# Turns, weight copies, head norms and final stores reordered in a three-block transformer kernel

## The reference, cut to what matters

```python
def first_block(x, ...):                       # blocks 1 and 2 (layers 0 and 1)
    for i in range(2):
        hn = rmsnorm(h, norm_mix[i])
        mix = diff_attention(hn, ...) if i == 0 else neighborhood_attention(hn, ...)
        h = h + mix
        h = h + swiglu(rmsnorm(h, norm_ffn[i]), w_gate, w_up, w_down)     # hidden 2816
        gate = sigmoid(rmsnorm(h, norm_ple[i]) @ ple_w_gate[i])
        h = h + gate * (p[i] @ ple_w_proj[i])
...
# in diff_attention: two softmax maps a head, a[0] - lam * a[1], then
    o = rmsnorm(o, subln) * (1.0 - lam_init)   # a norm per head of 128 values ("head norms")
    return o.reshape(B, S, D_MODEL) @ w_o
...
def second_block(x, meta_tokens, ...):         # block 3
    h = concat([meta, x])                      # 16 meta tokens ahead of the 256
    q, k, v, f_logit, b_gate, c_gate, u = split(rms_norm(h) @ w_in)
    y_attn = forgetting_attention(q, k, v, log_f)             # 8 heads of 64
    y_conv = b_gate * causal_depthwise_conv(c_gate * u, conv_w)    # width 3
    y = concat([head_rms_norm(y_attn), head_rms_norm(y_conv)])
    h = h + y @ w_out
    h = h + square(relu(rms_norm(h) @ w_ff1)) @ w_ff2         # hidden 4096
    return rms_norm(h)[:, 16:]
```

## Time and profile before

| | before |
|---|---|
| time, median of 3 runs | 1049.91 us (1049.12 to 1051.7) |
| profiled execution | 1049.74 us |
| its span in the trace | 1047.8 us |
| mean granted clock of TensorE | 0.989 |
| PE busy | 1004.1 us, 5549 matmuls |
| VectorE, ScalarE busy | 643.9 us, 497.6 us |
| moved by DMA | 174.78 MB, mean 167 GB/s |

### The profile page before, as it was taken

The page is one execution under the profiler, slowest core; times in us unless marked ns, Lnnn a source line. Parts: engine busy times, 40 slices in busy tenths (PEclk is TensorE's granted clock), DMA queues, the critical chain, the costliest instruction groups (busy, mean ns, idle before and its releaser), DMA issues.

```text
span 1047.8 us, 13887 instructions
## 1 busy us (share of the span) xinstructions
PE 1004.1 (96%) x5549; PEld 857.5 (82%) x5549; DVE 643.9 (61%) x990; ACT 497.6 (47%) x728; POOL 126.4 (12%) x207
## 2 busy tenths in 40 slices
PE   6998799999999999999999999999999899999996
PEld 5988678888888898887888888888889778888885
DVE  6766667655566775554665555578654777555553
ACT  6465445444443655454544444455654354444431
POOL 5000399620000000000000000012500000000000
PEclk9899899999999999999999999999999999999998
DMA  9833368956556454333376655545642237555510
GB/s 268 279 121 123 89 150 197 272 193 201 167 195 196 159 190 159 121 121 95 133 239 196 193 176 194 198 138 176 202 145 97 81 121 244 197 164 197 192 50 40
DMA packets 112575, 174.78 MB, mean 167 GB/s; under 512 B 5944, under 2 KB 73536, under 8 KB 112512
## 3 DMA queue, kind: packets, MB, share of 16 engines
q1 hardware_dynamic: 106224, 165.69, 49.5%
q0 software_dynamic: 6272, 8.21, 3.3%
q10 hardware_dynamic: 16, 0.00, 0.0%
HBM read 172.83 MB, written 1.05 MB: 166 GB/s over the span
## 4 chain that ended last, share of the span: by engine, by line
PE 79%; DVE 10%; ACT 6%; issue 3%; DMA 1%; SPq 0%; DVEq 0%; ACTq 0%
PE bank L902 24%; PE bank L904 24%; PE bank L903 24%; DVE wl L1358 4%; ACT wh L582 2%; PE bank L1090 2%; ACT prob L658 1%; PE bank L1012 1%; DMA raw<-in_da_w_qkv_dram 1%; DVE prob L1463 1%; PE bank L917 1%; PE bank L1067 1%; PE bank L1042 1%; ACT pt L675 1%; DVE xl L1426 1%
## 5 line engine op out<-in xcount | busy, mean ns | idle before, releaser
L1358 DVE TENSOR_TENSOR wl<-raw,wh 128x2048 fp32r<-128x2048 f32 x154 | 355.4, 2314 | 229.2 <-ACT wh L582 229.1
L582 ACT ACTIVATE wh<-raw 128x2048 fp32r<-128x2048 f32 x154 | 292.0, 1910 | 107.5 <-PE bank L904 102.1
L902 PE MATMUL bank<-wh,xh 128*128 128x512 f32 (+1 forms) x792 | 302.0, 381 | 5.7 <-DVE xl L1426 4.8
L903 PE MATMUL bank<-wl,xh 128*128 128x512 f32 (+1 forms) x792 | 296.5, 374 | 0.0
L904 PE MATMUL bank<-wh,xl 128*128 128x512 f32 (+1 forms) x792 | 296.4, 374 | 0.0
L902 PEld LDWEIGHTS bank<-wh,xh 128*128 128x128 f32 x792 | 149.8, 189 | 31.8 <-issue 5.4
L904 PEld LDWEIGHTS bank<-wh,xl 128*128 128x128 f32 x792 | 149.5, 189 | 27.4
L903 PEld LDWEIGHTS bank<-wl,xh 128*128 128x128 f32 x792 | 149.9, 189 | 25.3
L902 PE MATMUL bank<-wh,ah 128*128 128x512 f32 x320 | 127.4, 398 | 0.0
L904 PE MATMUL bank<-wh,al 128*128 128x512 f32 x320 | 125.1, 391 | 0.0
L903 PE MATMUL bank<-wl,ah 128*128 128x512 f32 x320 | 124.8, 390 | 0.0
(11 more groups left out here) (227 smaller groups left out, 900.0 us busy)
## 6 DMA issues: line engine op xcount, KB each, us to landing
raw<-in_w_ff_dram SPq DMA_DIRECT2D x32, 1024.0 KB, 5.2
raw<-in_ffn_w_gate_dram SPq DMA_DIRECT2D x44, 512.0 KB, 4.1
raw<-in_ffn_w_up_dram SPq DMA_DIRECT2D x44, 512.0 KB, 5.0
raw<-in_ffn_w_down_dram SPq DMA_DIRECT2D x22, 1024.0 KB, 5.0
raw<-in_na_w_qkv_dram SPq DMA_DIRECT2D x12, 1024.0 KB, 5.3
raw<-in_w_in_dram SPq DMA_DIRECT2D x12, 1024.0 KB, 5.2
raw<-in_da_w_qkv_dram SPq DMA_DIRECT2D x11, 1024.0 KB, 11.3
raw<-in_ple_w_gate_dram SPq DMA_DIRECT2D x8, 1024.0 KB, 5.1
```

The lines of the kernel that those rows point to most:

```text
L582: nc.scalar.activation(wh[:, i % RING, :], raw[:, i % RAW, :], ACT.Copy).then_inc(s_hi, 1)
L902: nc.tensor.matmul(dst, lh, rh, start=start, stop=False, skip_group_check=True)
L903: nc.tensor.matmul(dst, lh, rl, start=False, stop=False, skip_group_check=True)
L1358: nc.vector.tensor_tensor(wl[:, i % RING, :], raw[:, i % RAW, :], wh[:, i % RING, :].bitcast(F32), ALU.subtract).then_inc(s_lo, 1)
```

## The change

The diff has six parts.

1. Front. `first_turn_hi`, `first_turn_lo` and `split_blocks` are taken apart: the first half of x is turned into banks of its own (`first_bank`), ACT and DVE work through single blocks in an order mixed with the quarters of unit 0, and PE waits for single blocks (`first_lo`). PE's meta turn moves from behind the first pair to behind the first keys, its copies with it.
2. Attention in blocks 1 and 2. ACT's `split_to` of a slot is issued ahead of that slot's attention steps. The turn copies of the first half of the heads (`turns_hi`, `turns_lo`) are issued behind step TAIL.
3. Head norms of block 1. Three of four groups go to ACT (`head_norms(c, b)`, a copy with a scale, in place), the fourth stays on DVE; the factor `subln` leaves them and becomes the scale of the turn copies (`sub_col`); `head_roots(0)` is issued ahead of the slot's subtraction.
4. Block 3. `STEPS_2` has one step per unit of 128 features (two slots a weight unit), the tables of what happens in which slot follow, and one subtraction of the output weights (`split_to(first["wo", 2] + 3)` instead of + 4) is issued behind the products with the b gate.
5. End. The gain of the final norm is multiplied in half by half by DVE as the sums come (`add_scale`, as in the other norms), and behind the root DVE and ACT scale two halves each.
6. Four stores of 128 x 512 instead of two of 128 x 1024.

The core of the diff:

```diff
-        STEPS_2 = [[], [0], [1, 2]] + [[2 * n - 3, 2 * n - 2] for n in range(3, 11)] + [[]] * 4
+        STEPS_2 = [[], [0], [1, 2]] + [[s] for s in range(3, 19)] + [[]] * 8
...
-            return first["in", "v"] + 1 if slot < 3 else first["in", "c"] + (slot - 3) // 2
+            return first["in", "v"] + 1 if slot < 3 else first["in", "c"] + (slot - 3) // 4
...
-            for b in range(TB):
-                wait(sp, normed, "fin2", b, 1)
-                sp.dma_start(out[0].rearrange("(b p) n -> p b n", p=P)[:, b, :], hn[:, b, :]).then_inc(s_store, 16)
-            sp.wait_ge(s_store, 16 * TB)
+            for c in range(2):
+                for b in range(TB):
+                    sp.wait_ge(s_final[b], c + 1)
+                    cols = slice(512 * c, 512 * c + 512)
+                    sp.dma_start(out[0].rearrange("(b p) n -> p b n", p=P)[:, b, cols], hn[:, b, cols]).then_inc(s_store, 16)
+            sp.wait_ge(s_store, 16 * 2 * TB)
...
+            def split_block(u, k):
+                nc.scalar.activation(wh[:, u, 512 * k:512 * k + 512], raw[:, u, 512 * k:512 * k + 512],
+                                     ACT.Copy).then_inc(s_hi, 1)
...
             act.wait_ge(s_gturned, 1)
             nc.scalar.activation(gain_cols[:, :], bank[3][:, 0:KD], ACT.Copy).then_inc(s_gcols, 1)
             act.wait_ge(s_gcols, 1)
-            for b in range(TB):
-                first_turn_hi(b, 0)
-            split_blocks(0)
+            wait(act, turned, "mix0", 0, 0)
+            for k in range(4):
+                gained_hi(0, 0, k).then_inc(first_hi.sem, 1)
+            wait(act, turned, "mix0", 1, 0)
+            for k in range(4):
+                gained_hi(1, 0, k).then_inc(first_hi.sem, 1)
+                if k == 2:
+                    continue
+                for at in (2, 3) if k == 3 else (k,):
+                    act.wait_ge(s_first[at], 16)
+                    split_block(0, at)
             for b in range(TB):
                 first_turn_hi(b, 1)
-            split_blocks(1)
+            act.wait_ge(s_raw[1], landed[1])
...
 
+                def head_norms(c, b):
+                    wait(act, head_root, c)
+                    for m in range(4):
+                        dst = hn[:, b, 512 * c + P * m:512 * c + P * (m + 1)]
+                        at = 8 * c + 4 * b + m
+                        ins = nc.scalar.activation(dst, dst, ACT.Copy, scale=hst[:, at:at + 1])
+                    ins.then_inc(heads0.sem, 1)
...
+                if l == 0:
+                    wait(act, turned, "meta", 0, 0)
+                    nc.scalar.activation(xh[:, :, X0 - META:X0], bank[7][:, 0:P].rearrange("p (k s) -> p k s", k=KD),
+                                         ACT.Copy).then_inc(turned_hi.sem, 1)
                 for slot, steps in enumerate(STEPS):
                     part, c = part_of_slot(slot)
+                    split_to(first[part, l, c] + 4)
...
-                    split_to(first[part, l, c] + 4)
                     if slot % 2 == 1 and part == "q":
                         q_out(c)
                     if slot % 2 == 1 and part == "v" and l == 0:
                         v_copy(c)
-                turns_hi(f"att{l}", 0)
+                    if slot == 15 and l == 0:
+                        for b in range(TB):
+                            head_norms(0, b)
                 for s in range(TAIL, 19):
                     attention_step(l, s)
+                    if s == TAIL:
+                        turns_hi(f"att{l}", 0)
                     if s == 16:
                         split_to(first["wo", l] + 4)
                 if l == 1:
                     split_to(first["wo", l] + 1 + 4)
+                else:
+                    head_norms(1, 0)
                 turns_hi(f"att{l}", 1)
...
             for slot, steps in enumerate(STEPS_2):
-                if slot in (9, 11):
-                    attention_squares((slot - 9) // 2)
+                if slot in (13, 19):
+                    attention_squares((slot - 13) // 6)
...
                     wait(act, added, "dn2", c, b)
-                    square("fin2", b, c, hn[:, b, 512 * c:512 * c + 512])
+                    square("fin2", b, c, prob[:, 2 * c + b, :] if (c, b) != (1, 1) else pt[:, 0, :])
+            act.wait_ge(s_froot, 1)
+            for c in range(2):
+                cols = slice(512 * c, 512 * c + 512)
+                wait(act, normed, "fin2", 1, c)
+                nc.scalar.activation(hn[:, 1, cols], hn[:, 1, cols], ACT.Copy,
+                                     scale=rstd[:, 19:20]).then_inc(s_final[1], 1)
 
...
-                    for b in range(TB):
-                        need("mix0", b, kh)
                     for k in range(4):
+                        for b in range(TB):
+                            if kh == 0:
+                                wait(pe, first_lo, k, b)
+                            elif k == 0:
+                                need("mix0", b, 1)
...
-                    for c in range(2):
-                        for b in range(TB):
-                            pe.wait_ge(s_x[b], 16)
-                            turn(mix, b, c)
+                    for b in range(TB):
+                        pe.wait_ge(s_x[b], 16)
+                        if b == 1:
+                            pe.wait_ge(s_gcols, 1)
+                        for k in range(4):
+                            ins = nc.tensor.transpose(first_bank(b, k), h[:, b, k * P:(k + 1) * P], ident[:, :])
+                        ins.then_inc(turned.sem, 1)
+                    for b in range(TB):
+                        turn(mix, b, 1)
...
-                    meta_turn()
                 else:
                     first_unit(features_unit(u, 0, pair(0), True, x_cols, mix, fine=True), mix, (1, 2))
                     run(features_unit(u + 1, 1, pair(0), True, x_cols, mix))
                 spread_root(mix, bank[4])
                 run(quarter("k", 0))
 
+                if l == 0:
+                    meta_turn()
                 pe.wait_ge(s_emb, 16 * (l + 1))
...
                 link(nc.vector.tensor_scalar(m, m, 1.0 / (P * g2), EPS_HEAD / g2, ALU.mult, ALU.add))
-                inv_root(hst[:, 8 * c:8 * c + 8], m)
-
-            def head_norms(c):
...
+
+            def head_norms(b):
+                wait(dve, head_root, 1)
+                for m in range(4):
+                    dst = hn[:, b, 512 + P * m:512 + P * (m + 1)]
+                    ins = nc.vector.tensor_scalar(dst, dst, hst[:, 8 + 4 * b + m:9 + 4 * b + m], None, ALU.mult)
+                ins.then_inc(heads1.sem, 1)
 
             def head_sums(g):
...
-                first_turn_lo(b, 0)
-            split_blocks(0)
+            wait(dve, first_hi, 3, 0)
+            for k in range(4):
+                gained_lo(0, 0, k).then_inc(first_lo.sem, 1)
+            for k in range(4):
+                wait(dve, first_hi, k if k < 2 else 3, 1)
+                gained_lo(1, 0, k).then_inc(first_lo.sem, 1)
+                split_block(0, k)
             for b in range(TB):
                 first_turn_lo(b, 1)
-            split_blocks(1)
+            for k in range(4):
+                split_block(1, k)
+            split[0] = 2
             split_to(3)
...
+                if l == 0:
+                    wait(dve, turned_hi, "meta", 0, 0)
+                    nc.vector.tensor_tensor(xl[:, :, X0 - META:X0], bank[7][:, 0:P].rearrange("p (k s) -> p k s", k=KD),
+                                            xh[:, :, X0 - META:X0].bitcast(F32), ALU.subtract).then_inc(turned_lo.sem, 1)
...
                 for slot, steps in enumerate(STEPS):
                     part, c = part_of_slot(slot)
                     for s in steps:
                         attention_step(l, s)
+                    if slot == 14 and l == 0:
+                        head_roots(0)
                     split_to(first[part, l, c] + 4)
                     if slot % 2 == 1:
                         {"q": q_over_rms, "k": k_out, "v": v_out}[part](c)
-                    if slot == 14 and l == 0:
-                        head_roots(0)
...
                 for s in range(TAIL, 19):
                     attention_step(l, s)
+                    if s == TAIL:
+                        turns_lo(f"att{l}", 0)
...
-                if slot == 9:
+                if slot == 14:
                     head_sums(0)
-                if slot == 11:
+                for s in steps:
+                    attention_step(2, s)
+                if slot == 19:
                     head_sums(1)
                     attention_heads()
-                if slot != 11:
+                    convolve(2)
+                    convolve(3)
+                elif slot < 22:
                     split_to(unit_of_slot(slot) + 4)
-                for s in steps:
...
+            split_to(first["wo", 2] + 3)
...
-            r_ = row_roots("fin2", EPS_2)
-            for b in range(TB):
-                norm("fin2", b, r_[:, b:b + 1])
```

(5 more changed lines are left out.)

## The result

The changed kernel took 1026.50 us, median of 4 runs (1025.57 to 1026.79), against 1050.62 us before: ratio 0.9768, 95% interval [0.9756, 0.9781], faster. Measured twice more beside the kernel before, on other occasions, the ratio was 0.9783 [0.9768, 0.9799] and 0.9792 [0.9774, 0.9810]. The mean of the three is 0.9781, 23.0 us less. The forecast was 19.6 us less: 1030.3 us from 1049.91, with a range from 1026.5, which is 23.4 us less. By the first medians the gain is 24.1 us, beyond that range and 23% more than forecast; by the two traces it is 22.8 us, 16% more and inside it.

A forecast was written before the change was run, and what follows sets the result against it. TensorE, busy 96% of the span, was taken to bound the kernel by its work, waits and half-clock stretches; terms from -0.5 to +6.3 us summed to 19.6 us, giving 1030.3 us from 1049.91, with a range of 1026.5 to 1038.

The forecast's parts named there:

- the front: Start to first scores: scores 1.7 us earlier, but a new 4.0 us wait and a 2.2 us clock fall; -0.5 us.
- the third block: Block 3: single steps +2.1, large wait +2.1, no clock fall +1.4, last turn +0.65; together +6.3 us.
- the two places that the forecast named: Clock fall expected behind the wait at the first scores; possible behind the wait ahead of the first output product, +-1.4 us.
- The chain that "the change leaves alone": Ahead of the first keys: ACT's copy waiting 3.39 us for a transfer, 1.92 us of copy, 2.29 us of VectorE's subtraction.
- First attention block: Block 1: small waits +1.5, last quarter's keys and clock fall +5.1, head norms -0.1, tail +2.1 us.
- The tail's 2.1 us: End of block 1: turn copies behind step 14 spare the last scores 2.27 us; 2.0 us new wait at output product.
- Second attention block: Block 2: waits for pt (0.73) and keys (0.74) go, tail waits shrink to about 0.65; +4.0 us.
- the steps in pairs: Block 3: one step per feature block removes seven waits of 0.28 us for ACT's copy; +2.1 us.
- The large wait: Block 3, at the turn copy: one subtraction moved cuts 3.29 us to 1.2 (+2.1), with no clock fall (+1.4).
- End: Final norm and stores: gain beside the sums, halves scaled on VectorE and ACT, four stores; +1.2 us, bounds 0.9 and 1.8.
- The rivals that re-form waits in the tails or the third block: Tails: late turn copies, 1036 us, chance 0.20. Third block: sixteen more changes at 0.15 us, 1034.7 us, chance 0.10.
- the slower one: Attention blocks: copies ahead of the exponentials hold them up, 30.4 us in two blocks, 1061 us; chance 0.04.

The follow-up runs named there:

- e_keys_first: Changed kernel with VectorE's first keys ahead of the subtraction of the fourth unit, in the first block: 1026.96 us against 1026.5 to 1028.0.
- e_step0_first: Changed kernel with VectorE's first keys and step 0's row maxima both ahead of its subtractions, in the first block: 1024.56 us against 1028.00.
- e_turns_ahead: Changed kernel with the first turn copies of ScalarE and VectorE ahead of step 14 again, in both attention blocks: 1029.07 us against 1026.5 to 1028.0.
- e_copy_behind: Changed kernel with ScalarE's weight copy of a slot behind that slot's attention steps again, in both attention blocks: 1035.59 us against 1027.76.
- e_pairs: Changed kernel with the steps of the third block in pairs again: 1031.10 us against 1026.5 to 1028.0.
- e_two_stores: Changed kernel with two stores of 128 x 1024 again, each when both halves of its block are scaled: 1028.88 us against 1026.5 to 1028.0.
- e_broadcast: Changed kernel with the load of the subln gain to all 128 partitions put back in GpSimd's queue, read by nothing: 1026.30 us against 1027.76.
- e_wo_both: Changed kernel with both subtractions of output weights ahead of the turn copies again: 1030.67 us against 1026.5 to 1028.0.
- e_blocks_together: Changed kernel, but PE waits for all eight first blocks of x before the first product: 1025.25 us against 1028.00.

## Why the prediction missed

The trace's gain is 3.2 us larger than forecast. Two terms of the sum were mis-sized, the front (1.9 us of it) and the third block (1.4 us); smaller misses on both sides nearly cancel. The falls of the clock came at the two places that the forecast named. Only the third block's miss is there in each of the three traces of the changed kernel: the front's gain (to the scores of step 1, 45.21 before) is 1.3, 0.4 and 0.1 us in them.

**Front, -0.5 forecast, +1.4 in the trace.** The mechanism was right (a new wait for the first keys in place of the removed one, and a fall behind it), the sizes were too dark. The scores came at 38.7 where 39.85 was written, as the unit landed 2.4 us earlier in this execution; in seven others they came at 39.6 to 40.1. That part of the gain is luck of one execution. The fall cost 1.4 us, not 2.2. Of the wait of 2 us at the spread of the roots 0.34 us is there, since the pair ended late; where it ended at 20.7 to 21.2 that wait was 2.0 to 2.3 us, as forecast. The chain that "the change leaves alone" was misread: I took the landing of the unit as its head, and two experiments (e_keys_first, e_step0_first) showed the subtraction's place in VectorE's order to be the bound. Costing the single blocks as a gain of 0.8 us at the pair's end was wrong in kind. The pair ended at 22.6 in this trace, since its products ran at 0.21 us each until 13.0, and at 20.7 in others, and the scores' start didn't follow it: what is won at the start is paid back in the wait for the keys.

**First attention block, 8.6 forecast, 8.0 measured.** The sum nearly held (7.1 in each of the two repeats, where the fall at the output product lasted 6.8 us), its parts did not; that it held is luck. The early copies did all that was put down to them. The tail's 2.1 us were put down to the turn copies behind step 14; undone alone, that move costs nothing in this block (e_turns_ahead), while the early copy undone alone brings 0.48 and 1.07 us of waits back in the tail (e_copy_behind). The 2.0 us of new wait ahead of the output product was forecast and came, 1.99 us, with its fall; head roots and norms cost nothing, as forecast.

**Not foreseen: 0.5 us** ahead of the first feed-forward, where PE had waited 0.37 us for VectorE's norms. Why that wait is gone was not tested.

**Second attention block, 4.0 forecast, 4.4 measured**, and **third block, 6.3 forecast, 7.7 measured.** The term that was mis-sized in every trace is the steps in pairs: the prediction put a gap at its shown length and nothing more, 2.1 us in all, and it is worth 3.25. A gap costs 0.14 us beyond itself, as e_pairs shows; the waits of the second block were priced too low in the same manner, and the terms written down for it add up to 3.85 us, not 4.0. The large wait fell to 1.08 us as forecast (1.2), with no fall.

**End, 1.2 forecast, 0.8 measured.** VectorE's two halves and ScalarE's two, and the issues of the stores:

```profile
1019.97 0.88 DVE L1953 TENSOR_SCALAR hn<-hn,rstd 128x512 f32<-128x512 f32 x2
...
1019.97 1.33 ACT L935 ACTIVATE hn<-hn,rstd 128x512 f32<-128x512 f32 x2 [2.26 <-DVE rstd L1431]
...
1020.48 1.83 SPq L439 DMA_DIRECT2D out_dram<-hn  x4
```

VectorE's halves took 0.44 us each (0.45 taken). A tensor_tensor of the same 512 columns, with one input in PSUM, takes 0.69 us. The Trainium skill, VectorE: DVE Perf Modes, "The perf-mode tier table", has fp32 tensor_scalar out of SBUF at twice the rate of tensor_tensor; here the ratio is 1.6 (0.44 to 0.69, and 0.36 to 0.56 for 384 columns), so the trace agrees in direction, and the measured times decide. The four issues took 1.83 us one behind the other, 0.46 each where 0.4 was taken, and the last ended 1.0 us behind the last half. It started 5.6 us behind PE's last product, where 5.4 was forecast and 6.5 was before. The 2.0 us fixed for each store, which the prediction takes from the Trainium skill, DMA: Bandwidth & Descriptors, "Anatomy of one DMA", are a fit over transfers issued by GpSimd, and these stores are SyncE's; no run here separates such a part. What the runs show is that four stores end 0.26 us earlier than two (e_two_stores).

**The rest**, 1.3 us between the traces' 22.8 and the first medians' 24.1, is within the scatter: the runs of the kernel before lie at 1048.7 to 1052.9 us. The rivals that re-form waits in the tails or the third block did not occur; the slower one neither.

## What to carry to other kernels

Where one engine is busy 98%, the price of its gap is the gap, the overlap lost with it (0.14 us here) and, where the clock falls, 1.4 us or more: add all three for each gap. Bringing an engine to a meeting point earlier was worth nothing here unless the other side came earlier too, and could cost a fall. Ask of each wait what small instruction it is for, and what large one without hurry stands ahead of it on that engine: three such swaps were worth 7 us (copy ahead of steps), 3.4 (keys and maxima ahead of subtractions) and 2 to 3.5 (turns ahead of squares) here.

## What the runs showed of the hardware

TensorE fell to half clock behind a wait of 2.37 us for the first keys in one trace, and with a wait of 2.33 us at the same place, in a kernel with one more load (e_broadcast), it did not; behind 1.99 us of wait ahead of the output product it fell in 11 traces and not in 2, behind 0.68 and 1.08 us in none. At the spread of the roots it fell behind a wait of 1.78 us (e_wo_both) and in no trace behind 1.97 to 2.30 us. So here the length of the wait alone doesn't tell whether a fall follows. The stretch at half clock lasted 3.4 or 6.8 us, in traces of the same program. In some executions the products of 256 columns ran at 0.21 us instead of 0.12 until 13 us into the span, though the profile's clock column has 1.00 there: its first record starts at 13.0 us in those of the changed kernel, at 16.6 in e_blocks_together, and at 7.8 to 8.8 us in the eight traces at full speed. The landing of one weight unit wandered by more than 2 us between executions of the same program (32.4, 34.6 and 34.9 us in its three traces).
